# Turned copies of x, the norm columns and the C matrices come laid out from memory; TensorE turns none of them

## The reference

```
def even_layer(x, g_norm, w_in, b_f, w_out):
    z = rms_norm(x, g_norm) @ w_in
    ...
    y = jnp.concatenate([ya * jax.nn.silu(ga), yb * jax.nn.silu(gb)], axis=-1)
    return x + y @ w_out
...
    y = (jnp.einsum('blgp,ghp->blgh', xr, c_re.astype(jnp.float32))
         - jnp.einsum('blgp,ghp->blgh', xi, c_im.astype(jnp.float32))
         + d.astype(jnp.float32) * uf)
```

## Time and profile before

| | |
|---|---|
| median of 3 runs | 774.57 us |
| span of the profiled execution | 773.1 us |
| PE busy | 764.9 us (99%) |
| DVE, ACT, POOL busy | 516.4, 409.7, 230.6 us |
| share of PE in the chain that ended last | 98% |
| DMA | 130.70 MB, 169 GB/s on average |

### The profile page before, as it was taken

One profiled execution on the slowest core, in us unless ns is written; L12 is line 12 of the kernel. 1 busy time (PEld: TensorE's weight loads), 2 busy tenths in 40 slices (PEclk: granted clock), 3 DMA queues, 4 the chain that ended last, 5 costly groups with the idle time before them and its releaser, 6 DMA issues.

```text
span 773.1 us, 12621 instructions
## 1 busy us (share of the span) xinstructions
PE 764.9 (99%) x5057; PEld 661.9 (86%) x5057; DVE 516.4 (67%) x775; ACT 409.7 (53%) x663; POOL 230.6 (30%) x182
## 2 busy tenths in 40 slices
PE   9999999999999999999999999999999999999997
PEld 7889987899877889987778888998888888888885
DVE  5748765665667648866457965788788676777553
ACT  6645357634487444343335545736857555556451
POOL 3031796750751000055019910126001111011010
PEclk9999999999999999999999999999999999999999
DMA  9899995397621654554545556440464556655741
GB/s 234 200 250 227 256 220 131 85 206 176 162 83 55 235 173 144 187 191 151 150 132 164 187 194 191 137 138 29 140 215 138 184 174 214 190 177 178 238 171 54
DMA packets 78140, 130.70 MB, mean 169 GB/s; under 512 B 4478, under 2 KB 28274, under 8 KB 77954
## 3 DMA queue, kind: packets, MB, share of 16 engines
q1 hardware_dynamic: 76640, 124.96, 55.8%
q0 software_dynamic: 1200, 4.83, 2.0%
q10 hardware_dynamic: 242, 0.11, 0.0%
HBM read 128.82 MB, written 1.06 MB: 168 GB/s over the span
## 4 chain that ended last, share of the span: by engine, by line
PE 98%; DVE 1%; ACT 1%; issue 0%; DVEq 0%; ACTq 0%
PE ps L1666 15%; PE ps L1670 15%; PE ps L1674 15%; PE ps L1724 10%; PE ps L1707 6%; PE ps L1711 6%; PE ps L1703 6%; PE ps L1732 5%; PE ps L1802 2%; PE ps L1818 2%; PE ps L1833 2%; PE ps L2187 1%; PE ps L2064 1%; PE ps L1595 1%; PE ps L2016 1%; PE ps L2072 1%
## 5 line engine op out<-in xcount | busy, mean ns | idle before, releaser
L1011 DVE TENSOR_TENSOR w_lo<-stage,w_hi 128x1024 fp32r<-128x1024 f32 x224 | 294.0, 1336 | 157.7 <-ACT w_hi L664 157.2
L664 ACT ACTIVATE w_hi<-stage 128x1024 fp32r<-128x1024 f32 x230 | 239.0, 1060 | 234.0 <-PE ps L1674 104.0
L1666 PE MATMUL ps<-w_hi,act_t 128*128 128x512 f32 (+1 forms) x368 | 100.4, 395 | 0.2 <-ACT act_t L691 0.2
L1674 PE MATMUL ps<-w_lo,act_t 128*128 128x512 f32 (+1 forms) x368 | 96.5, 385 | 0.0
L1724 PE MATMUL ps<-act_t,w_hi 128*128 128x512 f32 x352 | 84.1, 391 | 0.0
L1674 PEld LDWEIGHTS ps<-w_lo,act_t 128*128 128x128 f32 x368 | 68.1, 188 | 14.0
L1666 PEld LDWEIGHTS ps<-w_hi,act_t 128*128 128x128 f32 x368 | 66.5, 188 | 15.3 <-issue 2.5
L1670 PE MATMUL ps<-w_hi,act_t 128*128 128x512 f32 (+1 forms) x304 | 79.5, 384 | 0.0
L1724 PEld LDWEIGHTS ps<-act_t,w_hi 128*128 128x128 f32 x352 | 64.7, 188 | 12.7
L1670 PEld LDWEIGHTS ps<-w_hi,act_t 128*128 128x128 f32 x304 | 56.1, 188 | 11.6
L1703 PE MATMUL ps<-act_t,w_hi 128*128 128x256 f32 x416 | 58.9, 284 | 0.0
(11 more groups left out here) (384 smaller groups left out, 1167.3 us busy)
## 6 DMA issues: line engine op xcount, KB each, us to landing
stage<-in_even_w_in SPq DMA_DIRECT2D x62, 512.0 KB, 5.5
stage<-in_odd_w_in SPq DMA_DIRECT2D x48, 512.0 KB, 4.0
stage<-in_w_gate_up SPq DMA_DIRECT2D x44, 512.0 KB, 4.7
stage<-in_w_down SPq DMA_DIRECT2D x22, 512.0 KB, 4.3
stage<-in_even_w_out SPq DMA_DIRECT2D x16, 512.0 KB, 3.8
stage<-in_odd_w_out SPq DMA_DIRECT2D x16, 512.0 KB, 3.9
stage<-in_w_in SPq DMA_DIRECT2D x10, 512.0 KB, 3.8
stage<-in_w_out SPq DMA_DIRECT2D x8, 512.0 KB, 5.1
```

Of the source, the lines that this page charges most:

```text
L664: nc.scalar.activation(w_hi[:, u % RING, :], stage[:, u % RING, :], ACT.Copy).then_inc(hi_ready, 1)
L1011: nc.vector.tensor_tensor(w_lo[:, u % RING, :], stage[:, u % RING, :], w_hi[:, u % RING, :].bitcast(F32), ALU.subtract).then_inc(lo_ready, 1)
L1666: mm(out[:, b, :], a_hi(k)[:, tok[b]], hi[:, i, :], start=(k == 0), stop=False)
L1674: ins = mm(out[:, b, :], a_hi(k)[:, tok[b]], lo[:, i, :], start=False, stop=(k == k_tiles - 1))
```

## The change

The host lays out three more arrays: x with channels on partitions (`x_turned`), all vectors as 84 columns (`columns`), and both C matrices spread and turned (`c_turned`). `x_turned` is loaded in four pieces of two k tiles (256 KB each): one ahead of unit 0, one ahead of each of units 1, 2 and 3. ACT and DVE make `act_t` straight from it. x with tokens on partitions is still needed for the squares and the residual sum; it is loaded as two DMAs of 512 KB ahead of unit 5. The 16 transposes of x, the one of the vectors and the 8 of C are gone, as are POOL's four spreading operations and one of DVE's two copies of C. The row of the diagonal matrices is now made between units 5 and 6, `keep_busy` runs 10 matmuls, with none behind. DVE has all its operations on units 0 to 4 ahead of its wait for `rstd`.

```diff
-MASKS_AT, TABLES_AT = 20, 42
+X_AT, MASKS_AT, TABLES_AT = 5, 20, 42
 FORGET_AT, PARAMS_AT = 5, 12
-WARM_BEFORE, WARM_BEHIND = 8, 3
+WARM_BEFORE = 10
...
+            x_columns = t["x_turned"].rearrange("p (k n) -> p k n", k=KD)
+            def load_turned(i):
+                sp_eng.dma_start(x_turned[:, 2 * i:2 * i + 2, :], x_columns[:, 2 * i:2 * i + 2, :]).then_inc(x_turned_in[i], 16)
+            load_turned(0)
             for name, (first, units, per, _) in chunks.items():
                 for j in range(units):
                     u = first + j
-                    if u == 1:
-                        load_x(1, x_rest_in)
+                    if 1 <= u < 4:
+                        load_turned(u)
+                    if u == X_AT:
+                        for b in range(NB):
+                            sp_eng.dma_start(x[:, b, :], t["x"][b * P:(b + 1) * P, :]).then_inc(x_in, 16)
...
-            for i, name in enumerate(("ssm_c_re_2", "ssm_c_im_2")):
-                pool.dma_start(c_in[i][:], t[name].rearrange("(t q) n -> q t n", q=P)).then_inc(c_in_landed, 16)
+            pool.dma_start(c_both[:, :, :].rearrange("p c n -> p (c n)"), t["c_turned"]).then_inc(c_in_landed, 16)
...
+            def hi_of_x(k):
+                act.wait_ge(x_turned_in[k // 2], 16)
+                nc.scalar.activation(act_t[:, k, :], x_turned[:, k, :], ACT.Copy, scale=col[:, COL_EVEN + k:COL_EVEN + k + 1]).then_inc(act_hi, 1)
+            for j in range(HALVED):
+                for i in range(2):
+                    hi_of_x(2 * j + i)
+                    hi_of_half(j, i)
...
+            for j in range(HALVED, 4):
+                for i in range(2):
+                    hi_of_x(2 * j + i)
+                split_hi(j + 1)
+            split_hi(5)
             act.wait_ge(x_in, 16 * NB)
-            act.wait_ge(x_rest_in, 16 * NB)
             squares(0, lambda b: x[:, b, :], lambda b: junk[:, b, :])
-            split_hi(5)
...
-            lo_of_turned(4, 4, 4, COL_EVEN + 4, KD + 4)
-            split_lo(4)
+            split_lo(5)
+            dve.wait_ge(ident_in, 16)
             dve.wait_ge(rstd_ready, 1)
             spread(rstd[:, 0:2])
-            split_lo(5)
...
-            pe.wait_ge(x_in, 16 * NB)
-            turn_x(0)
-            keep_busy(WARM_BEHIND, 3)
             start_chunk(("ga", 0))
...
-            row_of_diag()
-            for name in (("ga", 1), ("gb", 0), ("gb", 1)):
+            start_chunk(("ga", 1))
+            for j in range(4):
+                if j == 2:
+                    row_of_diag()
+                tokens_unit(("ga", 1), j, x_hi, x_lo, KD)
+            for name in (("gb", 0), ("gb", 1)):
                 tokens(name)
```

More of the change, by code:

```diff
@@ L175, in build @@
         steps = sb("steps", [P, NC])
-        inv_freq, parity = sb("inv_freq", [P, ROPE_HALF]), sb("parity", [P, 2])
+        inv_freq = sb("inv_freq", [P, ROPE_HALF])
         N_ROWS = 5 * KD + 3 * CT + 2 * ST
-        rows = sb("rows", [P, P])
         col = sb("col", [P, N_ROWS])
@@ L222, in build @@
         pow_tmp_early = over("pow_tmp_early", 10240, [P, 2, 512])
[L223 to L224 removed]
+        x_turned = over("x_turned", 0, [P, KD, S])
         y_lo = over("y_lo", 0, [P, 16, S], F32R)
@@ L459, in _ @@
             pool.wait_ge(landed[1], 16)
-            for dst, src in ((inv_freq[:], t["inv_freq"]), (parity[:], t["parity"])):
-                pool.dma_start(dst, src).then_inc(tables_in, 16)
+            pool.dma_start(inv_freq[:], t["inv_freq"]).then_inc(tables_in, 16)
             pool.dma_start(bf[:], t["even_b_f"].rearrange("(h o) -> h o", o=1)).then_inc(params_in, 16)
@@ L689, in hi_of_turned @@
                 for k in range(tiles):
-                    act.wait_ge(turned, first + (k | 1) + 1)
+                    act.wait_ge(turned, first - KD + (k | 1) + 1)
                     nc.scalar.activation(act_t[:, at + k, :], ps[:, 4 * BANK + ((at + k) % 8) * S:4 * BANK + ((at + k) % 8 + 1) * S], ACT.Copy,
@@ L1066, in _, with lo_of_x @@
             nc.vector.memset(neg_half[:], -0.5).then_inc(fills, 1)
-            dve.wait_ge(col_turned, 1)
-            then(nc.vector.tensor_copy(col[:], ps[:, 0:N_ROWS]))
-            TT(col[:, COL_MIX:COL_MIX + KD], col[:, COL_MIX:COL_MIX + KD], col[:, COL_FINAL:COL_FINAL + KD], ALU.mult).then_inc(col_ready, 1)
[L1070 to L1077, removed]
-            lo_of_turned(4, 4, 4, COL_EVEN + 4, KD + 4)
-            split_lo(4)
+            def lo_of_x(k):
+                dve.wait_ge(act_hi, k + 1)
+                STT(act_t[:, KD + k, :], x_turned[:, k, :], col[:, COL_EVEN + k:COL_EVEN + k + 1], act_t[:, k, :].bitcast(F32), ALU.mult, ALU.subtract).then_inc(act_lo, 1)
+            dve.wait_ge(columns_in, 16)
+            for j in range(HALVED):
+                for i in range(2):
+                    lo_of_x(2 * j + i)
+                    lo_of_half(j, i)
+            next_unit[0] = HALVED
+            for j in range(HALVED, 4):
+                for i in range(2):
+                    lo_of_x(2 * j + i)
+                split_lo(j + 1)
+            TT(col[:, COL_MIX:COL_MIX + KD], col[:, COL_MIX:COL_MIX + KD], col[:, COL_FINAL:COL_FINAL + KD], ALU.mult).then_inc(col_ready, 1)
+            split_lo(5)
+            dve.wait_ge(ident_in, 16)
             dve.wait_ge(rstd_ready, 1)
             spread(rstd[:, 0:2])
-            split_lo(5)
             dve.wait_ge(params_in, 16 * 5)
-            dve.wait_ge(tables_in, 16 * 2)
+            dve.wait_ge(tables_in, 16)
             for a in range(2):
@@ L1786, in _ @@
             channels(("qa", 1))
[L1788 to L1793, removed]
             for name in (("ka", 0), ("ka", 1)):
@@ L2207, with turned_groups @@
          "final_norm"]
+def turned_groups(*parts):
+    out = np.zeros((2, SSM_N, len(parts), CT, 4, 2, SSM_C), np.float32)
+    for i, part in enumerate(parts):
+        by_group = part.reshape(CT, 4, 2, SSM_C, SSM_N)
+        for a in range(2):
+            out[a, :, i, :, :, a, :] = by_group[:, :, a].transpose(3, 0, 1, 2)
+    return out.reshape(P, len(parts) * CT * P)
 def kernel(**inputs):
@@ L2218 @@
     given = {n: _np.ascontiguousarray(inputs[n]).reshape(_MATRIX.get(n, (-1,))) for n in _INPUTS}
-    given["vectors"] = _np.concatenate([given[n].reshape(-1, P) for n in _ROWS])
+    given["columns"] = _np.ascontiguousarray(_np.concatenate([given[n].reshape(-1, P) for n in _ROWS]).T)
+    given["x_turned"] = _np.ascontiguousarray(given["x"].T.reshape(KD, P, S).transpose(1, 0, 2)).reshape(P, KD * S)
+    given["c_turned"] = turned_groups(given["ssm_c_re_2"], given["ssm_c_im_2"])
     given.update(constant_tables())
```

55 lines of the change are left out of this document (15 added, 40 removed).

## The result

The changed kernel takes 783.16 us (median of 4 executions, 781.10 to 783.71), against 774.59 for the kernel before on the same chip: a ratio of 1.0105, with an interval of 1.0093 to 1.0117. I had forecast 775.6 and a range that ended at 778.6. In what follows, the one execution that ran at a granted clock of 0.65 throughout (of e5_c_alone, 1081.95 us) is left out. The profiled execution took 783.71, its span is 781.9. Two things cost time: a wait with a cold clock at the head, and, which was in no term of my sum, hundreds of matmuls that each take 6 ns longer.

What follows compares the result with a forecast made beforehand. PE, busy 99% of the span, was taken to bound the kernel. Unit 6 starting 1.8 us later and C's -0.8 gave +1.0 us on the 773.1 span; with 1.5 us around it, 775.6, range 773.0 to 778.6.

Steps and rivals of the forecast that it cites:

- C, -0.8: Removing C's 8 transposes, which held PE from 78.93 to 79.73, takes 0.8 us off the end.
- The start: At PE's head, unit 0 begins at 5.5 to 6.5 instead of 7.61; gain offered up to 3.1 us.
- the limit stays: Loads at the head: unit 3's landing stays at 12.9; PE starts unit 2 at 12.1 to 12.7.
- The chain: From x's landing through squares, rstd, diagonals, parameters, exponentials and copy, PE starts unit 5 6.3 us later, at 24.5.
- the head start: PE's earlier start, up to 3.1 us, is lost in the idle time ahead of unit 5.
- X: Time when x by token has landed: 18.2 taken, between 16.8 and 19.2.
- the cold case: Rival: the wait ahead of unit 5 cools PE's clock, costing 1.5 to 2.8 us, about 777.8; chance 0.27.
- the warm one: Likeliest case: PE stalls ahead of unit 5 but the clock holds, 774.2 to 776.6; chance 0.48.
- X need only be 0.5 us earlier: Argument against the clock falling: an X 0.5 us earlier keeps the wait below anything shown to cool.
- Unit 6: PE starts unit 6 at 27.6 against 25.86 before: +1.8 us.
- X late: Rival: x slowed to 275 GB/s lands at 20.4, +3.2 us; with the colder clock 777.8 to 780; chance 0.10.

Runs made afterwards that it cites:

- e5_c_alone: The kernel before with only the part on C changed (C laid out from memory, 8 transposes gone): 774.24 us without the left-out execution, ratio 0.9991.
- after: The changed kernel itself, with the whole change made to the kernel before: 783.16 us, ratio 1.0105.
- e6_packed: e3_reorder with each of the four pieces of the turned x as one stretch of 256 KB: 775.09 us, ratio 1.0008.
- e10_packed_plain: e1_pad, order unchanged, with each piece of the turned x as one stretch of 256 KB: 778.01 us, ratio 1.0047.
- e1_pad: The changed kernel with an unused tile of 2 floats per partition, putting the work area back at a multiple of 64: 780.79 us, ratio 1.0077.
- e7_x_sooner: e1_pad with x by token loaded ahead of unit 4, not unit 5, and squares and diagonal matrices ahead of unit 4's copies: 777.13 us, ratio 1.0028.
- e4_warm: e1_pad with 14 matmuls of ones ahead of unit 5, order and wait unchanged: 777.46 us, ratio 1.0033.
- e2_before_shift: The kernel before with one unused tile moving its work area 32 bytes off a multiple of 64, no instruction changed: 778.38 us, ratio 1.0048.
- e3_reorder: e1_pad with unit 5's copies ahead of the wait for x, units 6, 7 and first gate ahead of the mixer's parameters: 776.32 us, ratio 1.0023.

## Why the prediction was wrong

Three things failed: when unit 3 and x land and how long the chain behind x is (+2.0 us for unit 5), the cold clock, which was left out of the sum (+1.7), and the dropped tiles, which were put at nothing (+3.7). The terms in order:

**C, -0.8.** Right in the trace: -0.78 in after (+5.59 to +4.81), -0.72 by itself.

**The start.** Unit 0 at 5.79 was inside 5.5 to 6.5. "Unit 3 landed at 12.9 behind 3 MB, and the same 3 MB stand ahead of it now, so the limit stays" failed. By 13 us as many bytes had come, but two of the 16 shares of each unit came late, so unit 3 landed at 15.8 and unit 2 started at 14.03. e6_packed and the other packed runs show that the layout of the turned x does this. Why rows of 2 KB every 8 KB do it and those of the kernel before (2 KB every 4 KB) do not, and why two shares, is not settled.

**The chain.** The mechanism was right (squares, `rstd`, diagonals, parameters, exponentials, unit 5) and the head start was lost in it, as forecast; e10_packed_plain shows that unit 5 follows x one for one. Two sizes were off: X was 19.40 and not 18.2, beyond my upper bound of 19.2, and the chain 7.1 and not 6.3 long. That puts unit 5 at 26.51 in place of 24.5, +2.0. That X was off by only 1.2 us was luck. I had unit 3 at 12.9 and 5.3 us from there to X; unit 3 came 2.9 us later, and X 3.6 us behind it. Part of it is also the single execution: with the same order, x landed at 18.6 in e1_pad.

In the chain I had added durations measured when DVE and POOL did not work at once. In after POOL clears `mixed` and issues a DMA just then, and DVE's operation on 8 columns (L1093) takes 0.57 us. In e7_x_sooner POOL's DMA comes behind them, and the two copies and L1093 take:

```profile
23.02 0.34 DVE L1090 COPY sp_ldt<-log_dt 64x16 f32<-64x16 f32 x2
...
23.48 0.17 DVE L1093 TENSOR_SCALAR neg_sink<-sink 128x8 f32<-128x8 f32 x1
```

The four profiles in which these operations fall on POOL's (after, e1_pad, e4_warm, e10_packed_plain) all have the long times, and the others the short ones. No run moved POOL's work by itself, so that it is the cause is likely and not tested.

**The clock.** I gave the cold case 0.27 and the warm one 0.48, because the wait sat on the edge of what the earlier trace rows show. It came, and cost 1.70 us by the starts (4.82 less 3.12), inside my 1.5 to 2.8; e4_warm measures 1.5. The step that failed is the weight: the cold case was the one to add to the sum. The argument "X need only be 0.5 us earlier" counted one direction alone: X was as likely to come later, and did. e7_x_sooner shows more: a clock can fall after 2.04 us of idle, so the earlier trace rows was never an edge. The Trainium skill's page "TensorE: Matmul & The Clock Gate", Part 1, spoke for the fall; the trace agrees (0.52 behind the wait).

**The unlisted term, +3.9.** I had costed the removed tiles at nothing without a sentence. They moved the work area by 544 bytes, and 568 matmuls of 512 columns became slower, from 226.9 to 233.1 ns from start to start: 568 x 6.2 = 3.5 us. e2_before_shift measured the term by itself, 3.7 us by the times and 3.6 in the trace. The rest of the 3.9 came in among the small matmuls near 510 us.

**The sum.** Unit 6: +1.8 forecast, +2.0 for unit 5's start and +1.7 for the clock on top makes +5.5 (measured 5.47). C takes 0.8, and 3.9 come in behind 84 us: +8.6 of PE's 8.7 at the end. Without the address term the time would have been near 783.2 - 3.7 = 779.5, an estimate: a cold clock with X late as well, both of which I had as rivals (777.8, and 777.8 to 780), and still beyond my range. With it no case of mine reached 783.

## What to carry to other kernels

A transfer that leaves the head of the queue comes in somewhere else, and so does its consumer. Ask what is queued behind the instruction that waits for it, and put the copies that the busiest engine needs ahead of that wait: here that was worth 3.2 us at the head, against the 0.7 us that the 8 transposes of C were worth in the trace. When an edit adds or drops a small tile, compare the start addresses of all stationary operands modulo 64 before and after. And when a wait of some four microseconds on PE is forecast, the cold clock behind it belongs into the likeliest case: the three waits of 3.8 to 4.1 us ahead of unit 5 all cooled it. When a wait is for a load, look at its last share and not at the rate of the queue alone.

## What the runs showed of the hardware

- A matmul of 512 columns whose stationary operand starts 32 bytes off a multiple of 64 took 395 ns, and 389 with the operand on it (start to start 233 and 227 ns). The two kernels with the area off it (after, e2_before_shift) showed the first, the eleven others the second, and one tile of 32 bytes led from either to the other. Whether the stationary operand itself is what counts was not separated from other tiles of the area.
- In after the clock fell behind the wait, not in it: 1.00 in 22.7 to 26.5, 0.52 in 26.9 to 30.3. Behind PE's last matmul it fell without any work to follow. It fell after waits of 3.79, 4.05 and 3.92 us (after, e1_pad, e10_packed_plain) and of 2.04 us in e7_x_sooner, and not after 2.17 in after.
- It also fell behind small matmuls (32 x 64) with 0.60 us of idle time among them, near 514 us in e1_pad: 1.6 us at the lower clock, of the 2.4 lost there. In after, with 0.16 us of idle time at the same place, it stayed at 1.00. e1_pad's four executions all showed the same mean clock of 0.994, while e3_reorder's and e4_warm's profiles had no fall there. What decides it stays open.
- Four loads of 256 KB whose rows lie 8 KB apart made two of the 16 shares late, theirs and those of the loads among them: the last piece landed 8.0 us after its issue in e3_reorder and 6.6 us with the pieces packed (e6_packed), at the same 2 KB packets. The last share of unit 3 came 2.9 us behind the 14th in after, and 0.1 to 0.5 us behind it in the four packed profiles.
